# Routed experts' results: kept by token and choice, read back by plain transfers

## The reference, cut to what matters

```python
top_p, top_i = lax.top_k(jax.nn.softmax(le_sel, axis=-1), TOP_K)
gate_w = p_gsel * top_p / jnp.sum(top_p, axis=-1, keepdims=True)
experts = g_sel[:, None] * EXPERTS_PER_GROUP + top_i
...
def run_block(args):
    xb, e = args
    return (jax.nn.silu(xb @ w_gate[e]) * (xb @ w_up[e])) @ w_down[e]

y = lax.map(run_block, (x_buf, blk_e)).reshape(total, d)
return jnp.zeros((n, d), h.dtype).at[tok_sorted].add(y[dest] * w_sorted[:, None].astype(h.dtype))
```

## Time and profile before

| | us |
|---|---|
| median of 3 runs | 3539.17 |
| lowest and highest run | 3532.72 to 3539.87 |
| profiled execution, span of its instructions | 3541.6 |
| expert stage of layer 0: last result store issued, next stage begun | 1162.92, 1197.81 |
| expert stage of layer 1: last result store issued, next stage begun | 2092.99, 2119.70 |

### The profile page before, as it was taken

The page is one execution under the profiler, slowest core; times in us unless marked ns, Lnnn a source line. Parts: engine busy times, 40 slices in busy tenths (PEclk is TensorE's granted clock), DMA queues, the critical chain, the costliest instruction groups (busy, mean ns, idle before and its releaser), DMA issues. The chain is left out here.

```text
span 3541.6 us, 49036 instructions
## 1 busy us (share of the span) xinstructions
PE 3123.9 (88%) x19227; PEld 2143.7 (61%) x19227; DVE 1464.5 (41%) x2575; ACT 761.2 (21%) x1477; POOL 236.1 (7%) x435
## 2 busy tenths in 40 slices
PE   6999999699887599977987659989999999899998
PEld 5833668333333498753333337767888777678886
DVE  4125564400000533842000016455555683655555
ACT  3013562211111301821111111142110211221101
POOL 0000040111111200001111110000000000000000
PEclk8999999799998699988998769999999998999998
DMA  7176831999999322339999973122343263133421
GB/s 255 44 294 194 189 44 26 357 419 419 419 419 411 135 72 63 82 138 394 419 419 418 419 282 117 60 65 72 97 128 84 35 107 61 37 84 95 118 78 54
DMA packets 351346, 675.09 MB, mean 191 GB/s; under 512 B 69651, under 2 KB 276596, under 8 KB 295735
## 3 DMA queue, kind: packets, MB, share of 16 engines
q1 hardware_dynamic: 335420, 635.42, 51.7%
q0 software_dynamic: 13664, 31.49, 2.5%
q10 hardware_dynamic: 2067, 5.48, 0.4%
HBM read 642.80 MB, written 45.09 MB: 194 GB/s over the span
## 5 line engine op out<-in xcount | busy, mean ns | idle before, releaser
L3755 ACT ACTIVATE ffn_mixed<-ffn_mixed 128x512 f32<-128x512 f32 x44 | 27.8, 632 | 393.6 <-DVE ffn_mixed L3676 393.6
L1988 DVE TENSOR_TENSOR moe0b_hidden<-moe0b_hidden,moe0b_wide_ps 64x512 f32<-64x512 f32 (+1 forms) x21 | 12.7, 603 | 230.4 <-ACT moe0b_hidden L1985 230.4
L1973 PE MATMUL moe0b_wide_ps<-moe_raw,moe0b_feats 128*64 128x512 f32 x208 | 96.4, 614 | 9.8 <-DMA moe_raw<-in_moe_w_up 9.8
L1988 DVE TENSOR_TENSOR moe1b_hidden<-moe1b_hidden,moe1b_wide_ps 64x512 f32<-64x512 f32 (+1 forms) x18 | 10.3, 573 | 217.8 <-ACT moe1b_hidden L1985 217.8
L1988 DVE TENSOR_TENSOR moe1b_second<-moe1b_second,moe1b_wide_ps 64x512 f32<-64x512 f32 (+1 forms) x18 | 10.3, 573 | 217.3 <-ACT moe1b_second L1985 217.3
L1988 DVE TENSOR_TENSOR moe0b_second<-moe0b_second,moe0b_wide_ps 64x512 f32<-64x512 f32 (+1 forms) x20 | 12.2, 611 | 205.7 <-ACT moe0b_second L1985 205.7
L1974 PE MATMUL moe0b_wide_ps<-moe_raw,moe0b_feats 128*64 128x512 f32 x208 | 96.7, 615 | 0.0
L3673 DVE TENSOR_SCALAR ffn_mixed<-ffn_gate_ps,all_cols 128x512 f32<-128x512 f32 x44 | 35.6, 810 | 145.1 <-PE ffn_up_ps L3605 141.1
L1496 DVE TENSOR_REDUCE attn_top<-attn_scores 128x1 f32<-128x768 f32 (+1 forms) x96 | 72.4, 776 | 38.1 <-PE attn_scores L1409 38.0
L1465 ACT ACTIVATE attn_probs_t<-attn_turned 128x512 f32<-128x512 f32 x112 | 63.4, 604 | 82.4 <-PE attn_turned L1423 82.4
L243 POOL CAST second_first_hi<-all_ahead 128x1024 fp32r<-128x1024 f32 x8 | 9.7, 1218 | 994.9 <-DMA all_ahead<-in_ffn_w_up 709.4
(11 more groups left out here) (999 smaller groups left out, 8760.1 us busy)
## 6 DMA issues: line engine op xcount, KB each, us to landing
moe_raw<-in_moe_w_gate SPq DMA_DIRECT2D x88, 1024.0 KB, 27.3
moe_raw<-in_moe_w_up SPq DMA_DIRECT2D x88, 1024.0 KB, 27.9
moe_raw<-in_moe_w_down SPq DMA_DIRECT2D x86, 1024.0 KB, 28.1
all_ahead<-in_ffn_w_up SPq DMA_DIRECT2D x88, 512.0 KB, 5.1
all_h<-in_moe_w_gate SPq DMA_DIRECT2D x26, 1024.0 KB, 27.2
all_h<-in_w_ada SPq DMA_DIRECT2D x23, 1024.0 KB, 6.6
all_h<-in_moe_w_down SPq DMA_DIRECT2D x21, 1024.0 KB, 28.1
ffn_down<-in_ffn_w_down SPq DMA_DIRECT2D x40, 512.0 KB, 3.6
```

What stands on the lines that cost most here:

```text
L1973: nc.tensor.matmul(wide_ps[n][LOW, :], x[:, c, :], gate[:, at], start=c == 0, stop=c == DC - 1)
L1988: return nc.vector.tensor_tensor(hidden[n][HIGH, 0:cols], hidden[n][HIGH, 0:cols], wide_ps[n][HIGH, 0:cols], ALU.mult)
L3755: nc.scalar.activation(mixed[s][:], mixed[s][:], ACT.Silu).then_inc(silu_ready, 1)
```

## The change

A result is now stored at row token + 1024 x choice of the buffer, which has 2048 rows. The table of slots carries token + 1024 x choice in place of the token: the constant `token` has a second half for the second choice, VectorE subtracts 1024 from rows of the second choice to get the token (`slot_token`), and doubles or quadruples the row to get the address of a half or quarter. Every row of the buffer that is read is written by the stage's own stores, so `clear_rows` and the wait for it are gone, and so are the tables `row_of`, `half_row` and `quarter_row`.

The combination's rows come by plain transfers that SP issues after its loop: one of 1 MB per tile of tokens, both choices side by side. Every tile has its own place, no ring. ACT scales the first choice; of tiles 3 and 5 (tile 3 alone in layer 1) it also scales the second, and POOL adds the two; of the others DVE does as before. PE turns two tiles into one group of four PSUM banks, and DVE adds 256 columns at a time to `x`.

```diff
-    k["token"] = (np.arange(TOK_T, dtype=np.float32)[None, :] * PART + np.arange(PART, dtype=np.float32)[:, None] + 1.0)
+    token = np.arange(TOK_T, dtype=np.float32)[None, :] * PART + np.arange(PART, dtype=np.float32)[:, None] + 1.0
+    k["token"] = np.concatenate([token, token + CHOICE], 1)
...
-Y_ROWS = -(-BLOCKS_MAX * SLOTS // PART) * PART
+CHOICE = 1024
+Y_ROWS = 2 * CHOICE
...
+            PAIR_COLS = 2 * PART
+            picked = [raw[n].rearrange("p (j d) -> p j d", j=2) for n in range(NT)]
+            mixed = [raw[NT + n // 2][:, n % 2 * D:(n % 2 + 1) * D] for n in range(NT)]
...
+            by_pool = range(3, NT, 2)
...
             @block.sync
...
                         for k in range(PIECES):
                             weights.load(sp, k, e, k, x_weights)
-                        sp.wait_ge(x_act, i * 3 + 3)
-                        rows = P.y_dram[bass.ds((i + MAIN) * SLOTS, SLOTS), :]
-                        sp.dma_start(rows[:, 0:BANK], hidden[1][LOW, :]).then_inc(x_stored, 16)
-                        sp.dma_start(rows[:, BANK:D], hidden[1][HIGH, :]).then_inc(x_stored, 16)
-                        sp.wait_ge(x_stored, i * 32 + 32)
+                        sp.wait_ge(x_stored, i * 16 + 16)
                         sp.sem_inc(x_done, 1)
+
+                all_stored(sp)
+                for t in range(NT):
+                    sp.dma_start(picked[t], y_pairs[t * PART:(t + 1) * PART]).then_inc(picked_in[t], 16)
 
             @block.gpsimd
...
-                pool.wait_ge(slots_taken, 3)
-                pool.wait_ge(P.rows_cleared, CLEARED)
+                pool.wait_ge(slots_taken, 7)
...
                 store(N - 2)
                 store(N - 1)
-                pool.wait_ge(used, 4 * N)
-                all_stored(pool)
-                for t in range(NT):
-                    if t >= RING:
-                        pool.wait_ge(mix_ready, t - RING + 1)
-                    for j in range(2):
-                        nc.gpsimd.indirect_dma_start(picked[t % RING][j], None, P.y_dram[0:BLOCKS * SLOTS, :],
-                                                     bass.IndirectOffsetOnAxis(ap=row_of[:, t, j:j + 1], axis=0)).then_inc(picked_in[t % RING], 16)
+                for n, t in enumerate(by_pool):
+                    pool.wait_ge(mix_scaled, n + 1)
+                    nc.gpsimd.tensor_tensor(mixed[t], mixed[t], picked[t][:, 1, :], ALU.add).then_inc(mixed_by_pool, 1)
...
             @block.tensor
...
+                for m in range(NT // 2):
+                    if m >= 2:
+                        pe.wait_ge(mix_added, (m - 1) * DC)
+                    for t in (2 * m, 2 * m + 1):
+                        pe.wait_ge(*mixes_until(t))
+                        for c in range(DC):
+                            cols = slice(t % 2 * PART, (t % 2 + 1) * PART)
+                            last = nc.tensor.transpose(back_chunk(m, c)[:, cols], mixed[t][:, c * PART:(c + 1) * PART], P.ident[:])
                     last.then_inc(mix_turned, 1)
...
             @block.scalar
...
-                    nc.scalar.activation(mixed[t % 2], picked[t % RING][0], ACT.Identity, scale=weight[:, t, 0:1]).then_inc(mix_halved, 1)
+                    act.wait_ge(picked_in[t], 16)
+                    nc.scalar.activation(mixed[t], picked[t][:, 0, :], ACT.Identity, scale=weight[:, t, 0:1]).then_inc(mix_halved, 1)
+                    if t in by_pool:
+                        nc.scalar.activation(picked[t][:, 1, :], picked[t][:, 1, :], ACT.Identity, scale=weight[:, t, 1:2]).then_inc(mix_scaled, 1)
...
             @block.vector
...
-                V.scalar_tensor_tensor(slot_token[:], slot_ps, -1.0, unused[:], ALU.add, ALU.add).then_inc(slots_taken, 1)
+                V.scalar_tensor_tensor(slot_row[:], slot_ps, -1.0, unused[:], ALU.add, ALU.add).then_inc(row_found, 1)
+                dve.wait_ge(row_found, 1)
+                V.tensor_scalar(second_choice[:], slot_row[:], float(CHOICE), -float(CHOICE), ALU.is_ge, ALU.mult).then_inc(choice_found, 1)
+                dve.wait_ge(choice_found, 1)
+                V.tensor_tensor(slot_token[:], slot_row[:], second_choice[:], ALU.add).then_inc(slots_taken, 1)
...
+                for t in range(3):
+                    mix(t)
+                for m in range(NT // 2):
+                    dve.wait_ge(mix_turned, m + 1)
+                    at = first_tok + m * PAIR_COLS
                     w = int(at < CTX)
                     for c in range(DC):
-                        x = P.x[:, c, at:at + PART]
+                        x = P.x[:, c, at:at + PAIR_COLS]
...
+                    if 2 * m + 4 < NT:
+                        mix(2 * m + 4)
...
-def clear_rows(P, sp):
```

More of the change, by code:

```diff
@@ L390, in _ @@
             nc.vector.memset(P.eps[:, 1:2], LN_EPS).then_inc(eps_set, 1)
-            nc.vector.memset(P.zero[:], 0.0).then_inc(eps_set, 1)
             nc.vector.memset(P.cond[:], 0.0).then_inc(eps_set, 1)
@@ L1333, in grouped, with attention_stage @@
     return [make(t, t == 0, out if t == tiles - 1 else None) for t in range(tiles)]
-def attention_stage(nc, P, tag, turns, ahead=None, tables=None, store=None, also=None, windows=None, rows=None):
+def attention_stage(nc, P, tag, turns, ahead=None, tables=None, store=None, windows=None, rows=None):
     PIECE = 4
@@ L1670, in latent_mixer @@
         windows = WindowRows(nc, A, K, P, sb, sem)
-        attention_stage(nc, P, "attn", turns, ahead, store=distances, also=lambda sp: clear_rows(P, sp), windows=windows,
+        attention_stage(nc, P, "attn", turns, ahead, store=distances, windows=windows,
                         rows=[cq[:, 0], cq[:, 1], ckv[:, 0], ckv[:, 1]])
@@ L2104, in token_row @@
             def token_row(engine, j, t):
-                return engine.tensor_scalar(token_in_block[:, j, t, :], count[:, 0:BLOCKS], block_of[:, j, t:t + 1], token[:, t:t + 1],
+                return engine.tensor_scalar(token_in_block[:, j, t, :], count[:, 0:BLOCKS], block_of[:, j, t:t + 1], token[:, j * TOK_T + t:j * TOK_T + t + 1],
                                             ALU.is_equal, ALU.mult)
@@ L2165, in _, with store_halves @@
                 gather_pair(1)
-                pool.wait_ge(slots_taken, 3)
-                pool.wait_ge(P.rows_cleared, CLEARED)
+                pool.wait_ge(slots_taken, 7)
+                def store_halves(rows, places, into):
+                    nc.gpsimd.indirect_dma_start(y_halves, bass.IndirectOffsetOnAxis(ap=places, axis=0), rows, None,
+                                                 bounds_check=2 * Y_ROWS - 1, oob_is_err=False).then_inc(into, 16)
                 def store(s):
@@ L2333, in _ @@
                         last.then_inc(x_result, 1)
-                for t in range(NT):
-                    pe.wait_ge(mix_ready, t + 1)
-                    if t >= 2:
-                        pe.wait_ge(mix_added, (t - 1) * DC)
-                    for c in range(DC):
-                        last = nc.tensor.transpose(back[t % 2][c // HALF][:, c % HALF, :], mixed[t % 2][:, c * PART:(c + 1) * PART], P.ident[:])
+                for m in range(NT // 2):
[6 more added lines that the diff above has]
+                            last = nc.tensor.transpose(back_chunk(m, c)[:, cols], mixed[t][:, c * PART:(c + 1) * PART], P.ident[:])
                     last.then_inc(mix_turned, 1)
@@ L3845, in build @@
         P.y_dram = nc.dram_tensor("y_rows", [Y_ROWS, D], F32, kind="Internal").ap()
-        P.pool_sems = [[nc.alloc_semaphore(f"pool{l}_{n}") for n in range(8)] for l in range(DEPTH)]
+        P.pool_sems = [[nc.alloc_semaphore(f"pool{l}_{n}") for n in range(6)] for l in range(DEPTH)]
         both = [(slice(0, CTX), 1), (LAT, 0)]
```

101 lines of the change are left out of this document (40 added, 61 removed).

## The result

The changed kernel takes 3543.95 us (median of 14 runs, 3539.24 to 3553.96), the kernel before 3534.36 us (14 runs beside them, 3532.46 to 3544.63). The ratio is **1.0023, 95% interval 1.0015 to 1.0032**: slower by 8 us (0.0023 x 3534; the two medians stand 9.6 us apart), where the forecast had 15. The median of 3539.17 from which the forecast counted was of three runs and stands 4.8 us above that of the fourteen.

A forecast was written before the change was run, and what follows sets the result against it. TensorE (88% busy) was taken to bound the kernel, but at the expert stages' ends the engines wait for each other in turn. 10.0 + 5.1 = 15.1 us, counted from the median 3539.17, gave about 3554, range 3537 to 3561.

The forecast's parts named there:

- Late start, layer 0: End of layer 0's expert stage: first load waits for SyncE's spare-block loop, 0.65 us a pass, and goes out 11.4 us late.
- the clear: Attention stage: dropping the 32 zero stores that clear the row buffer counted as nothing, at most 2.2 us back.
- Late start, layer 1: End of layer 1's expert stage: first load waits for SyncE's spare-block loop, 0.50 us a pass, and goes out 3.8 us late.
- Landing: Loads at both stage ends: 5.7 us to the first, 2.74 us between tiles; tile 3 at 13.9, tile 5 at 19.4.
- Work on a tile: Both stage ends: GpSimd's addition 2.55 us, TensorE's eight transposes 1.97, additions into x 3.3 a pair.
- The sum: Both expert stage ends together: +10.0 us in layer 0 and +5.1 in layer 1, 15.1 us slower, about 3554.
- 36 t - 6.2: Loss over both stage ends at t us a pass of SyncE's spare-block loop; under 7 us for t below 0.37.
- the two combinations: First load to last addition at each expert stage's end: 1.5 us shorter in layer 0, 1.3 us longer in layer 1.
- the forecast case: Both expert stage ends get later, mostly by the late first loads: about 3554, own range 3545 to 3558; chance 0.72.
- A: SyncE's spare-block loop does not hold the loads at the stage ends: about 3539, no change; chance 0.13.
- B: Plain loads at the stage ends land slowly, 4.4 us apart: +28 us, 3567; chance 0.08.
- C: Less DMA traffic elsewhere, in the attention stage, helps more than shown, a gain of over 7 us: 3530; chance 0.07.

The follow-up runs named there:

- The padded kernel: The changed kernel plus 32 semaphore increments on SyncE that move nothing, in the attention stage where the zero stores stood; ratio 1.0028 (1.0017 to 1.0038).
- three loops skipped: The changed kernel with SyncE's, TensorE's and ScalarE's spare-block loops skipped when there is no spare block; ratio to the kernel before 0.9983 (0.9972 to 0.9994).

## Why the prediction was right in kind and wrong in size

- **Late start, layer 0: the step that failed.** The forecast said "I keep each layer's own rate" and took 0.65 us a pass, a first load 11.4 us late. It was 7.8 late (10.94 - 3.14), at 0.50 a pass. The rate was not the layer's. It belonged to the place of the loop in SyncE's program, and dropping the clear, the term costed at nothing, moved the loop out of that place. The forecast took each rate as fixed to its layer, and did not ask why the same loop with the same body ran at 0.65 in one layer and 0.50 in the other. That was the clue. The padded kernel, with nothing else changed, gives the forecast's 14.6 us back.
- **Late start, layer 1**: 3.8 forecast, 3.74 measured.
- **Landing**: 2.74 us from tile to tile was taken from a burst among other transfers. ScalarE's first scalings start from 1175.55 to 1188.37, 12.82 us over five steps, 2.56 each; that is the bound of 2.55 that the text had as its low end. Tile 5 came 0.9 us sooner than forecast for it, tile 3 0.5.
- **Work on a tile**: GpSimd's addition took 2.35 us (2.55 forecast), TensorE's turning 1.97 as said, the last additions of a pair 3.22 (3.3). From first load to last addition 28.4 and 23.6 us, forecast 30.0 and 24.6.
- **The sum**: by its formula, 36 t - 6.2, the measured passes (22 x 0.50 + 14 x 0.49 = 17.9) give 11.7; less 1.6 and 1.0 for the two combinations it is 9.1, and the traces give 8.8. Of the 6.3 us by which the forecast's sum was too high, 3.6 are the place of one loop and 2.6 the two combinations, in layer 0 mostly the landings. The absolute forecast, 3554, stands 10 us above the measured 3543.95; 4.8 of them are the median of three runs from which it counted. The measured time lies just below the forecast case's own range (3545 to 3558) and inside the wider one.
- **The clear**: its traffic cost the attention stage nothing, as said (224.72 us without it, 224.48 with it). Its 32 instructions were worth 3.7 us in the time of the first load.
- **Rivals.** A, the loop does not hold the loads: refuted, since skipping it brings 12.7 us. The Trainium skill's price for a compare-and-branch (Advanced Engine Details and Errata, Control Flow Timing, about 108 ns) gave an estimated 0.22 us for a pass of two; no engine's pass took less than 0.44 in any run here. B, slow landings: 2.56 us apart, not 4.4. C, a gain elsewhere: none in the attention stage, by the lengths just named, and TensorE's busy time in the two windows is the same within 0.4 us.

What stays open is what makes the place dear. The loop's body of loads is jumped over in every pass; the runs show a step from 0.50 to 0.65 us with 32 instructions added ahead of it and back with 96, in the two jumps across the body, and no more. The Trainium skill (Runtime: NRT & Kernel Launch, Instruction fetch mechanics) says that a program is fetched in blocks of 16 KiB; a jump across the edge of one would fit, but no run here shows where the edges lie.

## What to carry to other kernels

An engine that has nothing left to do still has its program to walk, and a transfer put at the end of it waits for that walk: look at the sequencer's branches there, not at busy time. Guard a loop that is mostly empty with one test outside it, or issue from a queue that is already past its own; here either turned 0.2% of loss into 0.1% of gain. And when the same code has two prices in one trace, find out why before using either.

## What the runs showed of the hardware

- The mean pass of a skipped loop has one price per engine in every run in which the engine walks it: 0.44 us on GpSimd and ScalarE, 0.53 on VectorE, 0.74 to 0.76 on TensorE. SyncE's alone had two, 0.49 to 0.50 and 0.65.
- VectorE's sum of tile 4 took 1.96 us at 1187.02 in the changed kernel, where the other sums took 1.28: it began while GpSimd's addition (1185.56 to 1187.91) was running and ended 1.07 us behind it. With three loops skipped the same overlap gave 1.95; without overlap, with SyncE's loop skipped, it was 1.28. The Trainium skill (SBUF — State Buffer, Who interferes with whom) says that a VectorE instruction with two SBUF inputs, as this one has, contends with a GpSimd instruction that reads SBUF, over a pair of ports that is an exclusive lock. The trace agrees that the two contend. A full stop until GpSimd's end is estimated from these rows at 0.89 + 1.28 = 2.17 us; measured is 1.96, so the sum was held up for most of the overlap, not for all of it.
- TensorE turned the last tile of layer 0 in 1.97 us at a granted clock of 0.50 (its 1.2 GHz level) in the changed kernel and in the one with the loads on GpSimd, and in 1.09 us at 1.00 (2.4 GHz) in the two that skip SyncE's loop. That is 0.9 us of the gain of these two, which no theory had counted. In the 17 us before, TensorE was busy 9.5 us with three loops skipped, 7.5 with SyncE's alone and 9.6 in the changed kernel, so these rows do not tell why the clock rose in the two and not in the other.
